# Two transformer blocks on one core: the end of the first mixer in another order, its softplus and mask in two halves

## The reference, cut to what matters

```python
def stick_breaking_attention(q, k, v):
        z = jnp.einsum('bthd,bshd->bhts', qb, k).astype(jnp.float32) * (D ** -0.5)
        mask = (key_pos[None, :] < tpos[:, None])[None, None]
        u = jnp.where(mask, jax.nn.log_sigmoid(-z), 0.0)
        between = lax.cumsum(u, axis=3, reverse=True) - u
        a = jnp.where(mask, jnp.exp(jax.nn.log_sigmoid(z) + between), 0.0)
        return jnp.einsum('bhts,bshd->bthd', a.astype(v.dtype), v)
...
        oa = rmsnorm(dsa_sparse_attention(qa, ka, va, qi, ki, wi, rel_bias), g_out_a[l])
        ob = rmsnorm(stick_breaking_attention(qb, kb, vb), g_out_b[l])
        o = jnp.concatenate([oa, ob], axis=-1) @ w_out[l]
        h = h + gate(1) * rmsnorm(o, g_post[l, 1])
```

## Time and profile before

| | |
|---|---|
| median of 3 runs | 1158.36 us (1152.35 to 1159.92) |
| the profiled execution's own time | 1158.58 us |
| its span in the trace | 1156.9 us |
| mean granted TensorE clock | 0.985 of full speed |
| PE busy | 1113.1 us, 96% |
| DVE busy | 812.2 us, 70% |
| ACT busy | 517.1 us, 45% |
| POOL busy | 47.3 us, 4% |

### The profile page before, as it was taken

How to read it: one execution, slowest core, us unless ns; L and a number is a source line. 1 busy time by engine, 2 the same in 40 slices (tenths; PEclk the granted TensorE clock), 3 DMA queues, 4 the chain that set the end, 5 groups by cost and what they waited for, 6 DMA issues and landing times.

```text
span 1156.9 us, 18061 instructions
## 1 busy us (share of the span) xinstructions
PE 1113.1 (96%) x7108; PEld 1005.8 (87%) x7108; DVE 812.2 (70%) x842; ACT 517.1 (45%) x602; POOL 47.3 (4%) x76
## 2 busy tenths in 40 slices
PE   7799999999988999999999999999999999999997
PEld 5699999879978789999979999998788887999996
DVE  4788898677674777677767787767765687555554
ACT  3244433454754553444455433445454445444432
POOL 1000000011020100000010000000100000000001
PEclk9999999999996999999999999999999999999999
DMA  8899997545421489897658999854553355666651
GB/s 323 327 388 384 368 373 264 191 156 168 146 73 37 146 298 308 311 320 253 217 210 318 346 334 336 272 169 147 190 182 109 110 182 174 212 215 226 217 174 55
DMA packets 144983, 266.95 MB, mean 231 GB/s; under 512 B 9657, under 2 KB 103974, under 8 KB 139686
## 3 DMA queue, kind: packets, MB, share of 16 engines
q1 hardware_dynamic: 143040, 262.96, 65.4%
q0 software_dynamic: 1056, 3.17, 0.8%
q10 hardware_dynamic: 838, 0.15, 0.1%
HBM read 263.60 MB, written 2.65 MB: 230 GB/s over the span
## 4 chain that ended last, share of the span: by engine, by line
PE 83%; DVE 7%; ACT 5%; DMA 2%; issue 1%; POOL 1%; SPq 1%; POOLq 0%; ACTq 0%; DVEq 0%
PE ps L1720 15%; PE ps L1723 14%; PE ps L1722 14%; PE ps L1676 11%; PE ps L1677 11%; PE ps L1678 11%; DMA w_raw<-in_w_ada 2%; DVE w_lo L1079 1%; ACT w_hi L739 1%; DVE nT L1091 1%; ACT nT_hi L739 1%; DVE nT L1291 1%; ACT nT L765 1%; DVE nT_lo L1098 1%; PE ps L2130 1%
## 5 line engine op out<-in xcount | busy, mean ns | idle before, releaser
L1079 DVE TENSOR_TENSOR w_lo<-w_raw,w_hi 128x2048 fp32r<-128x2048 f32 (+3 forms) x170 | 383.4, 2259 | 176.8 <-ACT w_hi L739 176.2
L739 ACT ACTIVATE w_hi<-w_raw 128x2048 fp32r<-128x2048 f32 (+3 forms) x170 | 319.7, 1885 | 275.7 <-PE ps L1678 143.9
L1720 PE MATMUL ps<-nT_hi,w_hi 128*128 128x256 f32 x1440 | 409.0, 284 | 2.5 <-DVE w_lo L1079 2.5
L1723 PE MATMUL ps<-nT_hi,w_lo 128*128 128x256 f32 x1440 | 408.2, 283 | 0.0
L1722 PE MATMUL ps<-nT_lo,w_hi 128*128 128x256 f32 x1440 | 408.1, 283 | 0.0
L1720 PEld LDWEIGHTS ps<-nT_hi,w_hi 128*128 128x128 f32 x1440 | 277.0, 192 | 5.5 <-DVE w_lo L1079 3.8
L1722 PEld LDWEIGHTS ps<-nT_lo,w_hi 128*128 128x128 f32 x1440 | 277.0, 192 | 1.4
L1723 PEld LDWEIGHTS ps<-nT_hi,w_lo 128*128 128x128 f32 x1440 | 276.9, 192 | 0.0
L1676 PE MATMUL ps<-w_hi,hT_hi 128*128 128x512 f32 x328 | 128.5, 392 | 0.0
L1158 DVE SCALAR_TENSOR_TENSOR arena<-arena,c_act 128x3072 f32<-128x3072 f32 (+2 forms) x49 | 128.1, 2650 | 0.0
L1677 PE MATMUL ps<-w_lo,hT_hi 128*128 128x512 f32 x328 | 128.1, 390 | 0.0
(11 more groups left out here) (255 smaller groups left out, 997.9 us busy)
## 6 DMA issues: line engine op xcount, KB each, us to landing
arena<-in_w_ada SPq DMA_DIRECT2D x16, 1536.0 KB, 7.7
arena<-in_ada_w SPq DMA_DIRECT2D x16, 1536.0 KB, 6.3
w_raw<-in_w_in SPq DMA_DIRECT2D x46, 512.0 KB, 4.6
w_raw<-in_w_ffn_down SPq DMA_DIRECT2D x44, 512.0 KB, 4.6
w_raw<-in_ffn_w_down SPq DMA_DIRECT2D x44, 512.0 KB, 4.3
w_raw<-in_w_ffn_gate SPq DMA_DIRECT2D x42, 512.0 KB, 5.9
w_raw<-in_w_ffn_up SPq DMA_DIRECT2D x42, 512.0 KB, 7.0
w_raw<-in_ffn_w_gate SPq DMA_DIRECT2D x42, 512.0 KB, 4.2
```

The costliest lines, as they stand in the source:

```text
L739: copy = lambda o, i: act.activation(o, i, ACT.Copy)
L1079: dve.tensor_tensor(lo(s, n), raw(s, n), hi(s, n).bitcast(F32), ALU.subtract).then_inc(lo_ready[s], 1)
L1720: pe.matmul(o, hi(s)[:, cols], nT_hi[:, kk, :], start=(half == first_half and k == 0 and i % 2 == 0), stop=False, skip_group_check=True)
L1723: last = pe.matmul(o, lo(s)[:, cols], nT_hi[:, kk, :], start=False, stop=(half != first_half and k == 3), skip_group_check=True)
```

## The change

It does six things. (1) The softplus on DVE and the mask on POOL are made for heads 0 to 3 and then for heads 4 to 7: two DVE instructions over half the columns, four POOL instructions over half of the heads each, and PE waits for a half at heads 0 and 4. (2) `value_half(6, 0)` stands ahead of the products that make `ob`. (3) The transposes of `ob` stand among the softmax's heads, ahead of head 6's, instead of ahead of all; ACT makes the high parts of `ob` ahead of its copy of head 7. (4) DVE copies the probabilities of heads 1 and 2 (`PT_DVE`), after its copies of `ob`; ACT squares `ob` in those places. `split_lo(*out1[1, 0])` stands behind DVE's eight heads. (5) The transposes of `oa` stand ahead of the whole of `out1[1, 1]`; ACT's `split_hi` of `out1[0, 0]` and `out1[0, 1]` stand behind the squares of `oa` and behind its high parts. (6) In every boundary `then()` stands ahead of `norm_hi(f, 1, ...)`.

```diff
@@ -21,6 +21,7 @@
 H = 8
+HALF = H // 2
 DH = 64
@@ -224,6 +225,7 @@
         osq_done = sem("osq_done")
+        pT_dve = sem("pT_dve")
         q_scaled = sem("q_scaled")
@@ -444,6 +446,15 @@
             e.wait_ge(rms_done, RMS.index(name) + 1)
+
+        PT_DVE = [1, 2]
+
+        def probs_ready(e, h):
+
+            if h in PT_DVE:
+                e.wait_ge(pT_dve, PT_DVE.index(h) + 1)
+            else:
+                e.wait_ge(pT_out, [g for g in range(H) if g not in PT_DVE].index(h) + 1)
 
@@ -712,9 +723,10 @@
             causal(diag(work), 2, OFF).then_inc(mask_ready, 1)
-            pool.wait_ge(u_ready, 1)
-            for c0 in (0, 2 * P):
-                causal(e_sb[:, :, c0:c0 + P], H, 0.0, True).then_inc(u_masked, 1)
+            for half in range(2):
+                pool.wait_ge(u_ready, half + 1)
+                for c0 in (0, 2 * P):
+                    causal(e_sb[:, HALF * half:HALF * half + HALF, c0:c0 + P], HALF, 0.0, True).then_inc(u_masked, 1)
             pool.wait_ge(a_exp, 1)
@@ -788,8 +800,8 @@
                 norm_hi(f, 0, range(2, PAIRS))
+                then()
                 norm_hi(f, 1, range(PAIRS))
-                then()
 
@@ -879,12 +891,12 @@
 
-            def out_squares(half, i):
-
-                for t in range(T):
-                    wait(act, osq_done, 2 * i + t - 1)
-                    act.activation(x_junk(t), y_row[:, t, half * NB:(half + 1) * NB], ACT.Square, scale=NB ** -0.5,
-                                   accum_out=stat[:, 4 + 2 * i + t:5 + 2 * i + t]).then_inc(osq_done, 1)
+            def out_square(half, i, t, s):
+
+                act.wait_ge(s, t + 1)
+                wait(act, osq_done, 2 * i + t - 1)
+                act.activation(x_junk(t), y_row[:, t, half * NB:(half + 1) * NB], ACT.Square, scale=NB ** -0.5,
+                               accum_out=stat[:, 4 + 2 * i + t:5 + 2 * i + t]).then_inc(osq_done, 1)
 
@@ -934,23 +946,24 @@
                                    accum_out=trig[:, 0, t, h:h + 1]).then_inc(p_exp, 1)
-            act.wait_ge(ob_out, T)
-            out_squares(1, 0)
             row_group(6, 0)
             for h in range(H):
-                if h == 4:
+                if h == H - 1:
                     for j in range(2):
...
                         copy(nT_hi[:, 4 + 2 * j:6 + 2 * j, :], ob_T[:, 2 * j:2 * j + 2, :]).then_inc(n_hi, 1)
-                act.wait_ge(p_tr, h + 1)
-                copy(e_sb[:, h, :], ps[:, 6 + h % 2, 0:CAUSAL]).then_inc(pT_out, 1)
+                if h in PT_DVE:
+                    out_square(1, 0, PT_DVE.index(h), ob_out)
+                else:
+                    act.wait_ge(p_tr, h + 1)
+                    copy(e_sb[:, h, :], ps[:, 6 + h % 2, 0:CAUSAL]).then_inc(pT_out, 1)
+            for t in range(T):
+                out_square(0, 1, t, oa_out)
             split_hi(*out1[0, 0])
-            act.wait_ge(oa_out, T)
-            out_squares(0, 1)
-            split_hi(*out1[0, 1])
             for j in range(2):
...
                 copy(nT_hi[:, 2 * j:2 * j + 2, :], nT[:, 2 * j:2 * j + 2, :]).then_inc(n_hi, 1)
+            split_hi(*out1[0, 1])
             split_hi(*gate_up("F1", 0, 0))
@@ -1399,7 +1412,9 @@
             dve.wait_ge(z_ln, 3)
-            dve.scalar_tensor_tensor(e_sb[:], z_sb[:], 0.0, e_sb[:], ALU.max, ALU.add).then_inc(u_ready, 1)
+            for half in range(2):
+                heads = slice(HALF * half, HALF * half + HALF)
+                dve.scalar_tensor_tensor(e_sb[:, heads], z_sb[:, heads], 0.0, e_sb[:, heads], ALU.max, ALU.add).then_inc(u_ready, 1)
             split_lo(*piece1(1, 6))
@@ -1410,8 +1425,6 @@
             for h in range(H):
-                if h == 4:
-                    split_lo(*out1[1, 0])
                 dve.wait_ge(l_mm, h + 1)
@@ -1421,9 +1434,13 @@
                 dve.sem_inc(lmax_ready, 1)
+            split_lo(*out1[1, 0])
             for t in range(T):
...
                 dve.tensor_copy(y_row[:, t, NB:2 * NB], ps[:, 2 + t, :]).then_inc(ob_out, 1)
+            for h in PT_DVE:
+                dve.wait_ge(p_tr, h + 1)
+                dve.tensor_copy(e_sb[:, h, :], ps[:, 6 + h % 2, 0:CAUSAL]).then_inc(pT_dve, 1)
             split_lo(*out1[1, 1])
@@ -1937,8 +1954,9 @@
 
-            pe.wait_ge(u_masked, 2)
             for h in range(H):
+                if h % HALF == 0:
+                    pe.wait_ge(u_masked, 2 * (h // HALF) + 2)
                 if h >= 4:
@@ -1964,6 +1982,7 @@
             logits(range(4, H))
+            value_half(6, 0)
 
@@ -1973,7 +1992,6 @@
             last.then_inc(ob_mm, 1)
-            value_half(6, 0)
 
@@ -1984,12 +2002,10 @@
 
-            pe.wait_ge(ob_ready, 1)
-            out_transposes(1, 2)
             pe.wait_ge(l_out, H)
...
             def probs_times_v(h):
-                pe.wait_ge(pT_out, h + 1)
+                probs_ready(pe, h)
                 v = [v_row[:, 0, s, h * DH:(h + 1) * DH] for s in range(2)]
@@ -1997,8 +2013,11 @@
             for h in range(H):
+                if h == 6:
+                    pe.wait_ge(ob_ready, 1)
+                    out_transposes(1, 2)
                 if h >= 2:
-                    pe.wait_ge(pT_out, h - 1)
+                    probs_ready(pe, h - 2)
                 pe.wait_ge(p_exp, 2 * h + 2)
@@ -2014,12 +2033,10 @@
             row_group(s0, banks[0], NB, None, 4, start=True).then_inc(w_used[s0], 1)
+            pe.wait_ge(o_ready, 1)
+            out_transposes(0, 6)
             weights(s1, use1)
-            row_group(s1, banks[1], NB, None, 4, start=True, ks=(0, 1))
-            pe.wait_ge(o_ready, 1)
-            pe.wait_ge(pT_out, H)
-            out_transposes(0, 6)
-            row_group(s1, banks[1], NB, None, 4, ks=(2, 3)).then_inc(w_used[s1], 1)
+            row_group(s1, banks[1], NB, None, 4, start=True).then_inc(w_used[s1], 1)
             pe.wait_ge(n_lo, TRB["O1"] + 4)
```

## The result

The changed kernel takes **1138.14 us** (median of 4 runs, 1137.20 to 1141.52), the kernel before in the same comparison 1156.84 us (4 runs, 1152.35 to 1159.92).

What follows compares the result with a forecast made beforehand. The prediction took PE to bound the kernel, busy 96% of the span. 14.9 us through the output projection, plus 2.5 for boundaries, less 3.2 for the clock, made 14.2 off 1158.58: 1144.4 us, range 1139.5 to 1150.

Steps and rivals of the forecast that it cites:

- The masks: First mixer's triangle products: with softplus and masks in halves PE begins earlier and keeps its clock; 4.6 us gained.
- From there to the heads: Between triangle products and softmax heads PE keeps its 4.6 us lead; the products of `ob` end at 350.5.
- The heads: Softmax heads: waits of 1.1 us for scaled `ob`, 0.8 for the last copy; last product at 361.8, 13.2 us ahead.
- were POOL ahead of the split, 0.4: Wait ahead of the transposes of `ob`: 0.4 us instead of 1.1 if POOL's power came before DVE's split.
- The output projection: First mixer's output projection: 22.9 us at the high clock level, ending at 384.7, 14.9 us ahead.
- The boundaries: PE's wait for a third weight piece goes in three boundaries, 0.8 us each; 2.5 us gained.
- The clock in the new heads: Softmax heads: the clock falls at the 1.1 us wait, slowing remaining heads and first projection matmuls; 3.2 us lost.
- the first rival: Softmax heads: the clock stays high through heads and wait; 1141.2 us, chance 0.17.
- The second: Softmax heads: the clock is low from the first head on, 6.2 us lost; 1147.4 us, chance 0.13.
- the fifth: Output projection: the low clock from the wait for `ob_ready` holds into the next stage; 1167 us, chance 0.02.
- The third: Softmax heads: the new order costs one more blocked 2.3 us at the wait, with slow clock; 1147 us, chance 0.12.
- the fourth: Masks: POOL's first pair ends as late as both did before, the 4.6 us are gone; 1149 us, chance 0.08.

Runs made afterwards that it cites:

- no_masks: The changed kernel with part 1 (softplus and mask in halves) undone; 1143.01 us, ratio to before 0.990.
- boundary_only: The kernel before with part 6 alone (weights' split ahead of the second rows' columns in each boundary); 1149.64 us, ratio 0.995.
- late_ob_1: The changed kernel with one DVE operation on 700 columns, changing nothing, added ahead of the signal that `ob` is scaled; 1140.06 us.
- late_ob_2: The changed kernel with one DVE operation on 1536 columns, changing nothing, added ahead of the signal that `ob` is scaled; 1141.78 us.
- masks_only: The kernel before with part 1 alone (softplus and mask in halves); 1146.39 us, ratio 0.993.
- before_2: The kernel before, unchanged, in another profiled execution; 1152.25 us.
- before_3: The kernel before, unchanged, in another profiled execution; 1153.49 us.
- before_4: The kernel before, unchanged, in another profiled execution; 1152.51 us.
- stand: The changed kernel with a wait of some 3.0 us added on PE after the transposes of head 0, without work; 1145.68 us, ratio 0.992.
- after_2: The changed kernel, unchanged, in another profiled execution; 1137.66 us.
- fill_wait: The kernel before with 14 unused 512-column matmuls in PE's 3.24 us wait for the scaled output; 1152.32 us, ratio 0.997.

## Why the prediction was wrong, step by step

**The masks, 4.6 us: right.** PE began at 323.47 (323.5 was given) and its eight heads ended at about 330.6 (330.5). no_masks measures the part at 4.55 us in the trace and 4.9 in medians.

**From there to the heads: right.** 350.5 was given, 350.37 is read.

**The heads: 0.36 instead of 1.1 us of wait for `ob`, 0.54 instead of 0.8 for the last copy.** The last product ended at 360.72 and not at 361.8. The walk put POOL's power behind DVE's split. In fact ACT's squares were done early enough for POOL to begin at 353.04, 0.14 us before the split. The case stood in the text ("were POOL ahead of the split, 0.4") and was not the one taken: 1.1 us off.

**The output projection: right.** 22.9 us given, 22.94 read (360.72 to 383.66), so 15.9 us ahead with the microsecond from the heads.

**The boundaries, 2.5 us: right in kind.** The three waits are gone and no new one stands in their place. boundary_only's first profile, with the same spell among the heads as before, has a span 5.0 us shorter; 1.7 of that is the spell near 598 us, which it hasn't, and 3.3 are left for 2.5.

**The clock in the new heads, 3.2 us lost: this step failed.** "I expect the fall there" rested on two readings. The first was that a wait of 1.1 us might lose the level; the wait was 0.36, and late_ob_1 and late_ob_2 kept the level over 1.28 and 2.15 us in the execution profiled of each. The second was that the heads' work, once slow, doesn't win it back, taken as a sign that such work can't hold it either. masks_only had it back among the heads after 3.4 us, before_2, before_3 and before_4 held it through the old heads behind the full stand-still, and the changed kernel held it through the new ones in three profiles of three. The loss was 0 instead of 3.2 us, and the first rival, 1141.2 us with a chance of 0.17, named the mechanism that came true. From 1144.4: 3.2 us for the clock and 1.1 us for the waits give 1140.1; the other 2 us to 1138.1 are the boundaries' 0.8 and 1.2 that I did not place.

**The range** ended at 1139.5, "just below the first rival", and left no room under it for terms of the walk that were small but all on one side: the rival kept the wait of 1.1 us, whose other end, 0.4, was in the text. That end should have stood in the range.

**The base.** The sum was taken off the execution at 1158.58 with the words that clock falls vary. Other executions show how much: with no spell in the heads the kernel before took 1152.3 to 1153.5, and the change is then worth some 14 us, not 20. That this is near the 14.2 us of the sum is chance: the sum counts a low clock in the old heads that these executions don't have. The medians of the comparison, 4 runs each, are 18.7 apart.

**The other rivals.** The second (low from the first head) and the fifth (the low level holds into the next stage) need a fall that none of the three profiles has. The third needs a wait for `ob` longer by 2.3 us than the 1.1 reckoned, where 0.36 was read; the fourth needs first masks that end near 326, where PE had them at 323.47.

## What to carry to other kernels

A stand-still of PE ahead of a stretch of work has two prices, its own length and the half speed that may follow it, and the second can be the larger: behind 3.24 us stood 20.5 us at the low level, some 10 us of time. When it was filled with products that nobody used, both the time and its spread shrank in the kernel before (4.5 us in 10 runs against 9.5 in 21), and in stand the time did. One profile shows one execution's clock: before a low stretch is taken into a sum, look at how far the kernel's times lie apart, since a loss that comes in some executions shows there first. When a part brings more alone than undoing it costs, suspect a cost that comes in some executions only, and look at the spread before the median.

## What the runs showed of the hardware

- The same stand-still of 3.24 us, in the same kernel at nearly the same place, was followed by the low clock in one execution and not in three. Its length alone does not decide: 1.28, 1.43, 2.15 and 2.34 us kept the high level, 2.85, 2.99 and 3.94 lost it, each in one profile, 3.24 did both, and 3.75 ahead of the triangle products lost it in all ten profiles that hold it. At a boundary 0.5 and 1.3 us close together lost it in some executions (579 us in the first profile after, none in after_2).
- How long the low level stays differs as much with PE busy throughout: in the heads of the first profile before until 377.9 us, 20.5 us; in stand until 364.2, 10.2 us; in masks_only until 358.5, 3.4 us.
- Filling PE's waits with products made the kernel before faster (fill_wait against before, 0.997, interval to 0.999) although it added 14 matmuls, 3.3 us of work.
- The level was lost near 256 us in every profile, with no wait of PE above 0.2 us from 238 us on, for 3.4 to 10.2 us. What PE did ahead of it each time were 48 products of only 72 columns, one every 0.11 us in the first profile before (249 to 254 us), and the clock fell among them or up to 1.2 us behind the last. This spell is the largest part of what sets the changed kernel's three profiles apart (3.4 us long at 1137.66, 10.2 at 1140.27).
